# Gate projections by seven products in the input stage, and a group's output projection inside the next group's scan

## What is computed

```python
def ssd_mixer(u, w_in, conv_w, conv_b, dt_bias, A_log, D, norm_w, w_out):
    proj = u @ w_in
    z = proj[..., :SSD_INNER]
    xbc = proj[..., SSD_INNER:SSD_INNER + SSD_CONV_DIM]
    dt_raw = proj[..., SSD_INNER + SSD_CONV_DIM:]
    xbc = jax.nn.silu(causal_depthwise_conv(xbc, conv_w, conv_b))
    ...
    y = ssd_chunked(xs, dt, A, Bm, Cm) + xs * D[:, None]
    y = y.reshape(b, s, SSD_INNER) * jax.nn.silu(z)
    yg = y.reshape(b, s, SSD_GROUPS, SSD_INNER // SSD_GROUPS)
    yg = yg * lax.rsqrt(jnp.mean(yg * yg, axis=-1, keepdims=True) + EPS)
    y = yg.reshape(b, s, SSD_INNER) * norm_w
    return y @ w_out
```

## Time and profile before

| | us |
|---|---|
| median of 3 runs | 2283.34 |
| lowest, highest | 2282.04, 2283.8 |
| the profiled execution | 2282.14 |
| its span | 2280.4 |
| TensorE busy in it | 2258.5 |
| VectorE, ScalarE, GpSimd busy | 1320.3, 1101.5, 1320.6 |

### The profile page before, as it was taken

How to read it: one execution, slowest core, us unless ns; L and a number is a source line. 1 busy time by engine, 2 the same in 40 slices (tenths; PEclk the granted TensorE clock), 3 DMA queues, 4 the chain that set the end, 5 groups by cost and what they waited for, 6 DMA issues and landing times.

```text
span 2280.4 us, 28960 instructions
## 1 busy us (share of the span) xinstructions
PE 2258.5 (99%) x10698; PEld 1845.5 (81%) x10698; DVE 1320.3 (58%) x1716; ACT 1101.5 (48%) x2016; POOL 1320.6 (58%) x950
## 2 busy tenths in 40 slices
PE   8999999999999999999999999999999999999998
PEld 6877888888888878888878888888888888888887
DVE  7357663333335798855568484747854343336777
ACT  4046544333333446655567474737643333334445
POOL 3224288777774664787734242334388777774654
PEclk9999999999999999999999999999999999999999
DMA  5100323323227855233263323232222323228744
GB/s 164 47 28 19 120 64 112 120 88 120 88 102 259 268 161 166 93 112 119 86 222 123 120 84 118 86 102 93 102 88 97 122 84 122 85 106 292 250 148 155
DMA packets 170807, 281.45 MB, mean 123 GB/s; under 512 B 19232, under 2 KB 104108, under 8 KB 168108
## 3 DMA queue, kind: packets, MB, share of 16 engines
q1 hardware_dynamic: 167084, 267.68, 34.9%
q10 hardware_dynamic: 3584, 11.93, 1.3%
HBM read 209.71 MB, written 69.86 MB: 123 GB/s over the span
## 4 chain that ended last, share of the span: by engine, by line
PE 92%; DVE 3%; POOL 2%; issue 1%; ACT 1%; DMA 1%; SPq 0%; ACTq 0%; DVEq 0%; POOLq 0%
PE ps L2212 44%; PE ps L1925 8%; PE ps L1927 8%; PE ps L1926 8%; PE ps L2302 5%; PE ps L2306 5%; PE ps L2298 5%; PE ps L2592 1%; PE ps L2582 1%; PE ps L2575 1%; PE ps L1948 1%; PE ps L2370 1%; POOL sq L1205 1%; PE ps L2135 1%; PE ps L2168 1%
## 5 line engine op out<-in xcount | busy, mean ns | idle before, releaser
L1051 POOL TENSOR_TENSOR s_lo<-s_val,s_hi 128x512 fp32r<-128x512 f32 x154 | 235.5, 1533 | 196.7 <-ACT s_hi L1575 196.0
L2862 DVE TENSOR_TENSOR xres<-ps,xres 128x512 f32<-128x512 f32 x132 | 90.5, 688 | 400.2 <-PE ps L2212 400.2
L947 POOL TENSOR_TENSOR w_lo<-w_raw,w_hi 128x1024 fp32r<-128x1024 f32 x50 | 119.3, 2387 | 270.6 <-ACT w_hi L1239 205.9
L972 POOL TENSOR_TENSOR p_lo<-p_val,p_hi 128x512 fp32r<-128x512 f32 x176 | 239.4, 1369 | 48.6 <-ACT p_hi L1380 37.5
L1380 ACT ACTIVATE p_hi<-p_val 128x512 fp32r<-128x512 f32 x176 | 111.0, 632 | 307.8 <-POOL p_val L998 307.8
L2212 PE MATMUL ps<-xn_hi,p_hi 128*128 128x512 f32 x704 | 189.0, 390 | 1.2 <-ACT xres L1483 1.2
L2212 PE MATMUL ps<-xn_lo,p_hi 128*128 128x512 f32 x704 | 188.2, 389 | 0.0
L2212 PE MATMUL ps<-xn_hi,p_lo 128*128 128x512 f32 x704 | 188.2, 389 | 0.0
L1575 ACT ACTIVATE s_hi<-s_val 128x512 fp32r<-128x512 f32 x154 | 97.0, 630 | 160.8 <-DMA d_val<-in_w_down 89.9
L1925 PE MATMUL ps<-xn_hi,w_hi 128*128 128x512 f32 x400 | 160.3, 401 | 0.0
L1926 PE MATMUL ps<-xn_lo,w_hi 128*128 128x512 f32 x400 | 156.0, 390 | 0.0
(11 more groups left out here) (361 smaller groups left out, 5570.3 us busy)
## 6 DMA issues: line engine op xcount, KB each, us to landing
s_val<-hidden SPq DMA_DIRECT2D x154, 256.0 KB, 2.9
hidden<-xres SPq DMA_DIRECT2D x20, 1792.0 KB, 6.5
wv_g<-in_w_gate SPq DMA_DIRECT2D x22, 1024.0 KB, 5.2
wv_u<-in_w_up SPq DMA_DIRECT2D x20, 1024.0 KB, 5.1
d_val<-in_w_down SPq DMA_DIRECT2D x70, 256.0 KB, 4.1
rows_v<-in_w_down SPq DMA_DIRECT2D x64, 256.0 KB, 3.8
mdec<-decay_sums SPq DMA_DIRECT2D x32, 512.0 KB, 4.2
xres<-parked_x SPq DMA_DIRECT2D x24, 512.0 KB, 6.0
```

The lines of the kernel that those rows point to most:

```text
L947: pool.tensor_tensor(w_lo[piece.slot][:, :], raw[piece.raw][:, :], f(w_hi[piece.slot][:, :]), ALU.subtract).then_inc(lo_done, 1)
L972: pool.tensor_tensor(p_lo[n][:, :, :], src, f(p_hi[n][:, :, :]), ALU.subtract).then_inc(p_lo_done, 1)
L1051: pool.tensor_tensor(s_lo[i][:, :], s_val[i][:, :], f(s_hi[i][:, :]), ALU.subtract)\
```

## The change

- **Gates in the input stage.** The gate blocks of groups 1 to 3 (six pairs) become blocks of the input stage, three rounds more (`NQ` = 9). Their rows take one SiLU on ScalarE instead of tap, three taps and SiLU, and are stored to `z_rows`; SP loads them back in halves for each group. Group 0's gates stay as fillers of its own scan.
- **Output as filler.** The output matmuls of group g-1 run as the two fillers of each chunk of group g's scan. The last group's come behind the scans, as before. The token halves of y and some weight pieces lie where xn lay.
- **VectorE between chunks.** A function `between(g, c)` on VectorE, placed behind the chunk's masked decay and ahead of the next chunk's `token_major`, has the output additions of group g-1 (two a chunk), the gate products, the adds of squares, the low parts (`rest`) and the reciprocals.
- **Squares.** VectorE adds the four blocks' squares, three adds a half; GpSimd adds none.
- **PSUM in place.** The masked C B^T stays in bank `CB` (no `cbm`), and TensorE waits for the masked decay of the chunk (`m_ready`) before it writes that bank for the next. y_diag + y_off is summed in bank `YDIAG`, and the y update reads it from there.
- GpSimd makes weight pieces' low parts in halves; ScalarE's high parts, splits and roots are placed between its chunks.

The diff, cut to its core:

```diff
-        Z_ORDER = [(b, half) for b in range(BG) for half in (1, 0)]
-        Z_PIECES, OUT_PIECES = range(BG), range(BG, 2 * BG)
...
+        ZU = 2 * BG
+        OUTS = 2 * NT
+        Z_ORDER = [(0, 0), (0, 1), (1, 0), (2, 0), (3, 0), (1, 1), (2, 1), (3, 1)]
+        Z_AFTER_CHUNK = [(5,), (6, 7), (8,), (9,), (10, 11), (12, 13), (14,), (15,)]
+        SILU_AFTER_CHUNK = {1: (0, 1), 3: (2, 3), 5: (4, 5), 7: (6,)}
+
+
+        def sums_after(g):
+            return {7: 0} if g == 0 else {3: 1, 6: 2} if g == 1 else {2: 2 * g - 1, 6: 2 * g}
+        FILL = [("z", u) for u in range(ZU)] + [("ssq", 0)]
+        for g_ in range(1, G):
+            for c_ in range(NT):
+                FILL += [("out", g_ - 1, 2 * c_), ("out", g_ - 1, 2 * c_ + 1)]
+                if c_ in sums_after(g_):
+                    FILL.append(("ssq", sums_after(g_)[c_]))
+        FILL += [("out", G - 1, 0), ("out", G - 1, 1)]
+
+        def fill_bank(*item):
+            return ps[:, (1, 0, 6)[FILL.index(item) % 3], :]
+
...
-        NQ = 6
+        NQ = 9
...
-        Q_BLOCKS = [(0, "x0"), (0, "x1")] + [(g, n) for g in range(1, G) for n in ("bc", "x0", "x1")]
+        Q_BLOCKS = ([(0, "x0"), (0, "x1")] + [(g, n) for g in range(1, G) for n in ("z0", "z1")]
+                    + [(g, n) for g in range(1, G) for n in ("bc", "x0", "x1")])
...
+                if is_z(i):
+                    sp.wait_ge(z_row_done, of_kind(i))
+                    sp.dma_start(z_rows[(g - 1) * BG + k - NCB], row_buffer(i)).then_inc(row_stored[i % 4], 16)
+                else:
+                    sp.wait_ge(row_done, of_kind(i))
+                    sp.dma_start(conv_rows[g * NCB + k], row_buffer(i)).then_inc(row_stored[i % 4], 16)
...
+            def load_z(g, half):
+                cols = slice(half * BANK, (half + 1) * BANK)
+                z_src = z_rows[(g - 1) * BG:g * BG].rearrange("r p s -> p r s")
+                sp.dma_start(zs_at, z_src[:, :, cols]).then_inc(z_loaded, 16)
...
+                    if c == 2:
+                        sp.wait_ge(z_gated, BG * 2 * g)
+                        load_z(g, 0)
+                        if g == 1:
+                            load_back(4, 5)
...
+                    if c == 5:
+                        sp.wait_ge(z_gated, BG * (2 * g + 1))
+                        load_z(g, 1)
+                        if not last:
+                            sp.wait_ge(y_split, BG * 2 * g)
+                            load_xrows(g + 1, 0)
+                        load_piece(g, 3)
...
+            def half_lo(piece, half):
+                slot, cols = piece.slot, slice(half * BANK, (half + 1) * BANK)
+                pool.wait_ge(hi_done, piece.count(1))
+                ins = pool.tensor_tensor(w_cols(slot, 1, half), raw[piece.raw][:, cols], f(w_cols(slot, 0, half)), ALU.subtract)
+                if half:
+                    ins.then_inc(lo_done, 1)
...
-                    for b in range(1, BG):
-                        pool.wait_ge(sq_ready, t.count("sq", BG * h + b + 1))
-                        if b > 1:
...
+                if is_z(i):
+                    act.activation(row_buffer(i), flat(row_banks(i)), ACT.Silu).then_inc(z_row_done, 1)
+                    return
...
+            def split(g, half):
+
+                at_ = half_place(g, half)
+                if (g, half) == (0, 0):
+                    act.wait_ge(z_full, 5)
+                elif (g, half) == (0, 1):
+                    act.wait_ge(z_full, ZU)
+                elif (g, half) == (1, 0):
+                    act.wait_ge(y_split, BG * 2)
+                elif (g, half) == (G - 1, 1):
+                    act.wait_ge(ydiag_full, NT * G)
+                else:
+                    act.wait_ge(out_full, out_count(g - 1, NT * (half + 1)))
+                for b in range(BG):
+                    act.wait_ge(z_gated, BG * (2 * g + half) + b + 1)
+                    src = yx_half(g, half)[:, b, :]
+                    act.activation(halves_sq[at_][b][:, :], src, ACT.Square).then_inc(sq_ready, 1)
+                    act.activation(halves_hi[at_][b][:, :], src, ACT.Copy, scale=gconst[:, g, GC_NW + b:GC_NW + b + 1])\
+                        .then_inc(y_hi_done, 1)
...
+                    if (g, c) == (1, 0):
+                        silu_z(ZU - 1)
+                        root(0)
+                    if (g, c) == (1, 2) or g >= 2 and c == 1:
+                        split(g - 1, 1)
+                    if (g, c) == (0, 6) or g and c == 5:
+                        split(g, 0)
+                    if c in PIECE_HI[g]:
+                        next_hi(g, PIECE_HI[g][c])
+                    if (g, c) == (1, 4):
+                        root(1)
+                    if g >= 2 and c == 3:
+                        root(2 * g - 1)
+                    if g and c == 7:
+                        root(2 * g)
                 t.add("chunk", NT)
                 t.add("carry", NT - 1)
                 t.add("loaded", 16 * NT // 2)
...
+            def token_major(k):
+
+                g, c = k // NT, k % NT
+                tok = slice(c * P, (c + 1) * P)
+                if c % 4 == 0:
+                    pe.wait_ge(rows_loaded[c // 4], 32 * (g + 1))
+                if k:
+                    pe.wait_ge(cb_freed, k)
+                    pe.wait_ge(m_ready, 2 * k)
+                ins = pe.matmul(ps[:, CB, 0:P], BT[:, tok], CT[:, tok], start=True, stop=True)
...
+                    else:
+                        pe.wait_ge(y_ready, k)
...
+                        for n in (2 * c, 2 * c + 1):
+                            out_part(g - 1, n, range(BG)).then_inc(out_full, 1)
+                    if c in sums_after(g):
+                        square_sums(sums_after(g)[c])
...
+            def token_major(k):
+
+                g, c = k // NT, k % NT
+                dve.wait_ge(cb_full, k + 1)
+                ins = dve.tensor_tensor(ps[:, CB, 0:P], ps[:, CB, 0:P], f(tri[:, :]), ALU.mult)
+                if c < NT - 1:
+                    if k:
+                        dve.wait_ge(states_full, t.count("carry", c) if c else (NT - 1) * g)
+                    ins = dve.tensor_copy(btok[:, :], ps[:, CB, P:2 * P])
+                ins.then_inc(cb_freed, 1)
...
+            def gated(g, half):
+
+                dve.wait_ge(y_ready, NT * g + 4 * (half + 1))
+                if g:
+                    dve.wait_ge(z_loaded, 16 * (2 * g + half - 1))
+                for b in range(BG):
+                    if g == 0:
+                        dve.wait_ge(z_done, Z_ORDER.index((b, half)) + 1)
+                    y = yx_half(g, half)[:, b, :]
+                    dve.tensor_tensor(y, z_of(g, b, half), y, ALU.mult).then_inc(z_gated, 1)
+
+            def square_adds(n):
+
+                s_ = halves_sq[half_place(n // 2, n % 2)]
+                dve.wait_ge(sq_ready, BG * (n + 1))
+                dve.tensor_tensor(s_[1][:, :], s_[0][:, :], s_[1][:, :], ALU.add).then_inc(sq_added, 1)
+                dve.tensor_tensor(s_[3][:, :], s_[2][:, :], s_[3][:, :], ALU.add).then_inc(sq_added, 1)
+                dve.wait_ge(sq_added, 2 * n + 2)
+                if n == 2 * G - 1:
+                    dve.wait_ge(ydiag_full, NT * G)
+                dst = sq_last if n == 2 * G - 1 else s_[3]
...
+            def rest(g, half, b):
+
+                n, at_ = 2 * g + half, half_place(g, half)
+                dve.wait_ge(y_hi_done, BG * n + b + 1)
+                if b < BG - 1 or n == 2 * G - 1:
+                    dve.wait_ge(sq_summed, n + 1)
+                else:
+                    dve.wait_ge(ssq_full, n + 1)
+                dve.scalar_tensor_tensor(halves_lo[at_][b][:, :], yx_half(g, half)[:, b, :],
+                                         gconst[:, g, GC_NW + b:GC_NW + b + 1], f(halves_hi[at_][b][:, :]),
+                                         ALU.mult, ALU.subtract).then_inc(y_split, 1)
...
+            def between(g, c):
+
+                if g == 0:
+                    if c == 6:
+                        gated(0, 0)
+                    if c == 7:
+                        square_adds(0)
+                        rests(0, 0, range(BG - 1))
+                    return
+                if c == 0:
+                    if g == 1:
+                        rest(0, 0, BG - 1)
+                    else:
+                        add_tile(g - 2, NT - 1)
+                        reciprocal_rms(2 * g - 2)
+                        gated(g - 1, 1)
+                elif (g, c) == (1, 1):
+                    reciprocal_rms(0)
+                elif (g, c) == (1, 5):
+                    reciprocal_rms(1)
+                elif g >= 2 and c == 4:
+                    reciprocal_rms(2 * g - 1)
+                if c:
+                    add_tile(g - 1, c - 1)
+                if (g, c) == (1, 1):
+                    gated(0, 1)
+                if (g, c) == (1, 3):
+                    square_adds(1)
+                if g >= 2 and c == 2:
+                    square_adds(2 * g - 1)
```

(35 more changed lines are left out.)

682 lines of the change are left out of this document (352 added, 330 removed), and 3 rows, old and new, of the table LO_AHEAD.

## The result

The changed kernel takes 2297.4 us (median; 2294.3 to 2298.3) where the kernel before takes 2283.4 (2282.0 to 2283.8): the ratio is 1.0057, 95% interval [1.0041, 1.0073], so it is slower by 14 us, more than the 0.2% named. The forecast was 2281.8 us, no change; the time lies above the range, 2267 to 2292, on the side that had a chance of 0.25. The profiled executions differ by 12.2 us in their spans (2292.6 and 2280.4): that of the changed kernel is the fastest of its four, 3.1 us under the median, so sums from its trace fall somewhat short of the median's loss.

A forecast was written before the change was run, and what follows sets the result against it. TensorE was taken as the bound, busy 99% of the span. 17.9 us removed against 16.4 us of stalls gave net -1.5 us: 2280.6 against the profiled execution, 2281.8 us as median forecast, range 2267 to 2292.

The forecast's parts named there:

- What leaves TensorE: Gate blocks: 72 fewer matmuls, 16.3 us less; squares no longer waiting for GpSimd, 1.6 us less; 17.9 us in all.
- SP's queue and the pieces: New waits on SP's queue ahead of later decay loads, and GpSimd's half pieces ahead of xds: costed at nothing.
- The new wait: TensorE's next token_major waits for VectorE's mask, with all work queued behind it; stalls summed to 16.4 us.
- Group 0's two one-filler chunks: Scan chunks with one filler of twelve matmuls, where the mask comes late: 0.65 us of stall each.
- Chunk 7 of group 0: Its mask is late because ScalarE does squares, high parts and a weight piece before its exponentials: a 5.1 us stall.
- Group 1's chunk 4: VectorE has rests and gates together between mask and next first operation, 5.8 us of extra work: 3.0 us stall.
- Tail: Behind the last group, the norm follows two additions, three adds and four rests: 0.7 us late for its transpose.
- The next group's first mask: After group 0's chunk 7, three adds and three rests on VectorE precede the next token_major: mask 2.3 us late.
- Groups 2 and 3: VectorE's adds, rests and gates between chunks stall TensorE 1.5 us in each group, 3.0 us in all.
- Rival 3: The 5.1 us stall halves TensorE's clock for a while, losing 3.7 us: 2285.5 us; counted within the forecast's 0.40 chance.
- Rival 2: VectorE becomes the bound, rests stretched beside GpSimd past a mean of about 0.95 us: 2291.8 us, slower; chance 0.25.
- Rival 1: The waits are mostly absorbed, stalls 6 us: 2271.4 us, or 2265.4 with no stalls; faster; chance 0.35.

The follow-up runs named there:

- e9: Changed kernel with weight pieces loaded first, C B^T product in SBUF without its wait, group 0's end reordered on ScalarE, rests after the next group's first mask: 2265.2 us.
- e11: e9 with seven of the eight sums of squares moved back from VectorE to GpSimd, at the end of its chunk: 2271.8 us.
- e1: Changed kernel with weight pieces asked for on SP's queue ahead of decay loads in group 0, ahead of gates and rows in groups 1 to 3: 2281.9 us.
- e8: Kernel before the change, with only the masked product left in PSUM and TensorE's wait for the mask before the next token_major added: 2296.2 us.
- e4: Changed kernel with nothing moved, TensorE doing transposes of the identity at the five longest waits to stay busy: 2292.0 us.
- after: The profiled execution of the changed kernel, without further edits: span 2292.6 us, where the kernel before has 2280.4.
- e6: Changed kernel with weight pieces first, product in SBUF without the wait, and group 0's squares and last piece's high part behind chunk 7's exponentials: 2269.9 us.
- e12: Changed kernel with weight pieces first and product in SBUF without the wait, plus 28 transposes before TensorE's one long wait: 2271.0 us.
- e10: e9 with the masked product in PSUM and TensorE's wait for the mask as the change has them: 2275.2 us.

## Why the prediction was wrong

- **What leaves TensorE (17.9 us): right.** e9 has all of the change but the PSUM product, with some work reordered, waits by record 1.0 us with the tail's, and lies 18.2 us under the kernel before. The 1.6 us for the squares cannot be split from it; e11 shows 4.4 us of wait at one place instead of the 1.6 at three.
- **SP's queue and the pieces, costed at nothing: the step that failed.** The text looked at the decays' landing times and at VectorE's signals, and not at the order "decay, gates, rows, piece" or at ScalarE, in whose queue the piece's high part stands ahead of the exponentials. It gave ScalarE 2 us of slack; ScalarE waited 2.83, 8.75 and 9.86 us for the three pieces. Undoing this one order (e1) brings 15.5 us of the 15.6 us by which the forecast missed (medians). It had said that a wait naming a DMA would be an error at the root; it came one engine further back, under ScalarE's name and not TensorE's.
- **The new wait: right in mechanism.** Group 0's two one-filler chunks: forecast 0.65 us each, measured 0.59 and 0.57 in e1, and 0.60 in e8. A wait of 0.75 us for chunk 2's mask, which ScalarE made late, was not forecast. Chunk 7 of group 0: 5.1 and 5.11. Group 1's chunk 4: 3.0 and 2.35. Tail: 0.7 and 0.61. The next group's first mask: 2.3, and 2.53 in e4. Groups 2 and 3 without late pieces: 3.0, and 0.95 in e1. The recorded stalls of e1 are 12.1 us with the tail's, where 16.4 was forecast; restarts and clock fill the gap, so that e1's 2281.9 beside the forecast 2281.8 is in part luck.
- **Rival 3, the clock: real, but one stall was counted and four falls came.** I gave 3.7 us for the 5.1 us stall (32 transposes at the rates of the earlier trace rows make 3.9). The chunk behind that stall held 2.8 us, and nothing of it net: it takes 9.24 us in e4 too, at the full clock, with the 2.53 us wait at its end. The other falls stand behind the late pieces, and keeping TensorE busy in all the long waits brought 5.4 us net. The Trainium skill (TensorE: Matmul & The Clock Gate, "What's actually happening") has idleness as what throttles; four of five waits above 2 us agree, and e4 above all. The waits of 2.35 us without a fall and of 0.56 and 1.19 us with one (windows at 0.78 and 0.66) show that the recorded wait is no measure by itself.
- **Rival 2, VectorE as the bound: wrong for this time, though its number (2291.8) was nearer.** The 32 rests took 25.0 us in after, a mean of 0.78, under the 0.95 it needed, and e1 did not touch VectorE. It is not nothing: e6 shows three rests at 3.60 us.
- **Rival 1 (absorbed): wrong as the change stands.** e9 shows what it would have taken: 2265.2, beside the 2265.4 named for no stalls.

What stays open: when exactly the clock falls, and what it costs net to better than some 2 us (5.4 by e4's medians; its profiled execution gives less, 1.9 us of span).

## What to carry to other kernels

When a change adds or reorders transfers on an issuing queue, walk each load to the first instruction that needs it and then ask what stands behind that instruction in its engine's own queue. Here a 512 KB piece that no one needed soon held up the exponentials that everyone needed, and moving a few lines of SP's order was worth 15.5 us. A wait that saves a small buffer (256 floats a partition) has to be priced against all chunks: 10 to 13 us here, most of it from waits under 0.9 us that are not worth a line in a list, and from restarts which no wait records.

## What the hardware showed that was not expected

- The granted clock can fall behind short gaps after thin work: 1.19 us, and 0.56 us, behind eight one-column matmuls (windows at 0.66 in e6 and 0.78 in e12), yet it stayed at 1.00 behind 2.35 us after dense projections, and behind the same eight matmuls without such a gap (e9). Four places are too few for a rule.
- A slow stretch is partly free: of 8 to 10 us, 5 came back as waits or were spent in the added transposes once the clock was held up (e4).
- Short waits cost more than their record: e8's span is 13.7 us longer with 11.1 recorded, e10's 11.3 with 7.2. Over the 16 or 17 chunk starts where TensorE's weight loads show idle time that is 0.15 to 0.3 us each; a single one in e10 shows 0.26.
- VectorE beside GpSimd: masks with one input in PSUM stayed at 673 to 690 ns in every run that has them, while an addition of squares with both inputs in SBUF took 1525 ns on average at its worst place and a pair of masks 2.81 us. The Trainium skill (SBUF — State Buffer, "SBUF: two separate sides") has a port pair that a GpSimd operation and a VectorE operation with two SBUF inputs share as an exclusive lock; the rows agree.
